# The last four experts of a mixture-of-experts layer, with expert 31's gate and up moved to the front

## The reference, cut to what matters

```python
for e in range(N_EXPERTS):
    hid = jax.nn.silu(t @ w_gate[e]) * (t @ w_up[e])
    out = out + combine[:, e:e + 1] * (hid @ w_down[e]).astype(f32)
```

## Time and profile before

| | |
|---|---|
| median of 3 runs | 1825.13 us (1824.73 to 1826.35) |
| the profiled execution | 1825.3 us, its span 1823.3 us |
| TensorE busy | 1663.8 us (91% of the span) |
| VectorE, ScalarE busy | 1034.6 and 387.7 us |
| mean granted clock of TensorE | 0.973 |
| the experts, in the 40 slices of the page | from slice 30 on the transfers run at 420 to 434 GB/s nearly throughout |

### The profile page before, as it was taken

One profiled execution on the slowest core, in us unless ns is written; L12 is line 12 of the kernel. 1 busy time (PEld: TensorE's weight loads), 2 busy tenths in 40 slices (PEclk: granted clock), 3 DMA queues, 4 the chain that ended last, 5 costly groups with the idle time before them and its releaser, 6 DMA issues.

```text
span 1823.3 us, 34390 instructions
## 1 busy us (share of the span) xinstructions
PE 1663.8 (91%) x14856; PEld 1334.9 (73%) x14856; DVE 1034.6 (57%) x2175; ACT 387.7 (21%) x993; POOL 0.2 (0%) x4
## 2 busy tenths in 40 slices
PE   7999999999999999999999999999998766566766
PEld 4555686888888886776899998778787555445554
DVE  1399979888867427787699884556433211111112
ACT  0254414211220104222322212203502100000001
POOL 0000000000000000000000000000000000000000
PEclk9999999999999999999999999999999978888899
DMA  9423334223240313744434443332398999999997
GB/s 383 180 82 115 110 135 162 105 112 129 104 150 24 127 47 137 268 164 162 174 139 180 185 168 139 139 122 104 137 421 320 431 434 426 432 431 431 431 426 298
DMA packets 30421, 395.00 MB, mean 217 GB/s; under 512 B 3296, under 2 KB 6624, under 8 KB 14432
## 3 DMA queue, kind: packets, MB, share of 16 engines
q1 hardware_dynamic: 30304, 393.31, 53.4%
HBM read 392.25 MB, written 1.05 MB: 216 GB/s over the span
## 4 chain that ended last, share of the span: by engine, by line
PE 82%; DMA 14%; DVE 3%; issue 1%; ACT 0%; SPq 0%; DVEq 0%
PE bank L2161 14%; PE bank L1871 13%; DMA arena<-w_moe 12%; PE bank L731 12%; PE bank L1599 7%; PE bank L4115 5%; PE bank L2438 3%; PE bank L2484 3%; PE bank L1029 2%; PE bank L4126 2%; PE bank L3869 2%; PE bank L2434 2%; PE bank L1334 1%; PE bank L785 1%; DMA ring<-w_moe 1%; PE bank L3091 1%
## 5 line engine op out<-in xcount | busy, mean ns | idle before, releaser
L1871 PE MATMUL bank<-arena,ring 128*128 128x256 f32 (+1 forms) x940 | 167.4, 336 | 0.0
L1871 PEld LDWEIGHTS bank<-arena,ring 128*128 128x128 f32 x940 | 148.0, 191 | 14.5 <-issue 0.4
L4115 PE MATMUL bank<-arena 128*32 128x128 f32 x1992 | 80.2, 332 | 76.9 <-DMA arena<-w_moe 73.4
L4281 DVE TENSOR_TENSOR arena<-arena,bank 128x128 f32<-128x128 f32 x32 | 9.2, 287 | 235.3 <-PE bank L4115 235.1
L4115 PEld LDWEIGHTS bank<-arena 128*32 128x32 f32 x1992 | 71.2, 137 | 84.3 <-DMA arena<-w_moe 77.5
L2161 PE MATMUL bank<-arena 128*128 128x256 f32 x504 | 115.7, 379 | 0.0
L731 PE MATMUL bank<-layer_input,ring 128*128 128x256 f32 x496 | 111.5, 381 | 0.0
L2161 PEld LDWEIGHTS bank<-arena 128*128 128x128 f32 x504 | 95.7, 190 | 13.2 <-DVE arena L2302 0.2
L731 PEld LDWEIGHTS bank<-layer_input,ring 128*128 128x128 f32 x496 | 92.8, 190 | 15.0 <-issue 2.8
L4115 PE MATMUL bank<-ring,arena 128*32 128x128 f32 x1920 | 64.8, 299 | 27.9 <-DMA ring<-w_moe 26.7
L4115 PEld LDWEIGHTS bank<-ring,arena 128*32 128x32 f32 x1920 | 59.2, 121 | 34.1 <-DMA ring<-w_moe 28.1
(11 more groups left out here) (572 smaller groups left out, 3162.1 us busy)
## 6 DMA issues: line engine op xcount, KB each, us to landing
arena<-w_moe SPq DMA_DIRECT2D x11, 6144.0 KB, 20.0
ring<-w_moe SPq DMA_DIRECT2D x11, 6144.0 KB, 20.4
ring<-w_ffn_in SPq DMA_DIRECT2D x13, 2048.0 KB, 7.6
ring<-w_moe SPq DMA_DIRECT2D x12, 2048.0 KB, 16.4
ring<-w_ffn_in SPq DMA_DIRECT2D x7, 3072.0 KB, 10.3
ring<-w_proj SPq DMA_DIRECT2D x7, 3072.0 KB, 9.8
arena<-w_moe SPq DMA_DIRECT2D x10, 2048.0 KB, 14.8
ring<-w_ffn_out SPq DMA_DIRECT2D x6, 2816.0 KB, 9.6
```

The source lines that it names most:

```text
L1871: last = eng.matmul(out, w[:, k * P:(k + 1) * P], x[:, k, :], start=(start and k == 0), stop=(stop and k == half - 1), skip_group_check=True)
L4115: ins = eng.matmul(bank[x][group[q], 0:P], xe[:, k, SLOTS * e:SLOTS * e + SLOTS], weight(e, first, last, (x * KT + k) * FE + q * P, P), st ...
```

## The change

In the last quad TensorE now begins with expert 31's gate and up, before the scatter of the quad before it; the turned hidden rows of expert 31 go to a place of their own (`last_hidt`, in `self.A`) and wait there for the down at the end. The scatter at expert 30 stands ahead of its gate. VectorE's and ScalarE's programs for the last quad are written out in the same order. The rest of expert 31's up is loaded ahead of the loop, to a sixth place (`up2`, in `self.A`). Its down goes to the place that held expert 2's down: three quarters in one transfer, the last quarter in 16 transfers of 8 partitions each. Eight fills are put ahead of the down of 29 and of 30, behind the wait for the copied rows and ahead of the wait for the weights; two fills ahead of each lone scatter. In the first attention the fills at the last pair go from 8 to 14.

```diff
-        sp.wait_ge(parts_used[1], LAST - 1)
-        self.load_part(sp, LAST, 0, 1, HELD_UP)
-        sp.wait_ge(parts_used[2], LAST - 1)
         self.load_last_down(sp)
...
+        self.load_held(sp, "up2", UPS // 2 + HELD_UP, UPS)
         with sp.Fori(0, (PARTS_AGAIN - WHOLE_FROM) // 2) as it:
...
-                sp.wait_ge(used, x - 1)
+                sp.wait_ge(used, x - 1 + (x == LAST - 1 and part < 2))
                 self.load_part(sp, x, (x - RESIDENT - 1) % 2, part)
...
+        place, split = self.kept_weights()["down"], (FET - 1) * D
+        sp.dma_start(place[:, 0:split], self.W["moe"][LAST][:, UPS:UPS + split]).then_inc(self.sem("first_in"), 16)
+        for r in range(0, P, 8):
+            sp.dma_start(place[r:r + 8, split:], self.W["moe"][LAST][r:r + 8, UPS + split:])\
+                .then_inc(self.sem("kept_in"), 16)
...
-                self.fill(pe, 8, b)
+                self.fill(pe, 14, b)
...
+            def last_quad(i):
+                x0, z = i * QUAD, QUAD - 1
+                project(0, z, last=True, copied=i * 2 + 1).then_inc(s["gate_done"], 1)
+                eng.wait_ge(self.sem("kept_in"), 9 * 16)
+                project(1, z, last=True).then_inc(s["up_done"], 1)
+                eng.wait_ge(s["y_dve"], x0 + 1)
+                eng.wait_ge(s["y_act"], x0 + 1)
+                for t in range(2):
+                    scatter(t)
+                eng.wait_ge(s["hid_ready"], x0 + 1)
+                eng.transpose(bank[3][:, 0:P], v["hid"], self.con("ident")).then_inc(s["hid_turned"], 1)
+                for e in range(z):
...
+                    if e == 2:
+                        eng.wait_ge(s["gwt_copied"], i * 2 + 2)
+                        eng.wait_ge(s["y_dve"], x0 + 3)
+                        eng.wait_ge(s["y_act"], x0 + 3)
+                        for t in range(2):
+                            scatter(t)
+                    eng.wait_ge(gate_in, arrived)
+                    project(0, e).then_inc(s["gate_done"], 1)
...
+                    eng.wait_ge(s["hidt_copied"], x0 + e + 2)
+                    eng.wait_ge(s["y_dve"], x0 + e + 1)
+                    eng.wait_ge(s["y_act"], x0 + e + 1)
+                    if e:
+                        self.fill(eng, 8, bank[0])
+                        eng.wait_ge(down_in, 64)
+                    down(e, False, True)
...
+                self.fill(eng, 2, bank[0])
+                eng.wait_ge(s["y_dve"], EXPERTS)
+                eng.wait_ge(s["y_act"], EXPERTS)
+                scatter_alone(2, 0)
+                eng.wait_ge(link, quads + 4)
+                scatter_alone(2, 1)
+                eng.wait_ge(self.sem("first_in"), 48)
+                down(z, False, True)
...
-            quad(quads - 1, last=True)
+            last_quad(quads - 1)
+            self.fill(eng, 2, bank[0])
             eng.wait_ge(s["y_dve"], EXPERTS + 1)
```

More of the change, by code:

```diff
@@ L4100, in weight @@
                 return self.kept_weight(at, n)
-            if last and e == QUAD - 1 and at < UPS // 2 + HELD_UP:
+            if last and e == QUAD - 1:
                 return self.held_weight(at, n)
@@ L4120, in down @@
         def down(e, first, last):
+            rows = last_hidt if last and e == QUAD - 1 else hidt
             for f in range(FET):
                 if last and e == QUAD - 1 and f == FET - 1:
-                    eng.wait_ge(self.sem("kept_in"), 9 * 16)
+                    eng.wait_ge(self.sem("kept_in"), (9 + P // 8) * 16)
                 for g in range(4):
-                    ins = eng.matmul(bank[2][group[g], 0:256], hidt[:, SLOTS * f:SLOTS * f + SLOTS],
+                    ins = eng.matmul(bank[2][group[g], 0:256], rows[:, SLOTS * f:SLOTS * f + SLOTS],
                                      weight(e, first, last, UPS + f * D + (g - e) % 4 * 256, 256), start=(f == 0),
@@ L4159, in moe, with quad @@
         if who == "pe":
-            def quad(i, first=False, second=False, last=False):
+            def quad(i, first=False, second=False):
                 x0 = i * QUAD
@@ L4223, in quad @@
                         eng.wait_ge(down_in, parts)
-                    down(e, first, last)
-                    if e == QUAD - 1 and not last:
+                    down(e, first, False)
+                    if e == QUAD - 1:
                         gather(i + 2)
@@ L4252, in moe, with silu, quad, last_quad @@
         if who == "act":
-            def quad(i, last=False):
+            def silu(n):
+                eng.wait_ge(s["gate_done"], n + 1)
+                eng.activation(v["sg"], bank[0][:, 0:P], ACT.Silu).then_inc(s["silu_done"], 1)
+            def quad(i):
                 for e in range(QUAD):
                     x = i * QUAD + e
-                    eng.wait_ge(s["gate_done"], x + 1)
                     if e:
                         eng.wait_ge(s["hid_ready"], x)
-                    eng.activation(v["sg"], bank[0][:, 0:P], ACT.Silu).then_inc(s["silu_done"], 1)
-                    if last and e == 2:
-                        eng.wait_ge(s["down_done"], x + 1)
+                    silu(x)
+                    copy_rows(x, e, eng.copy, (2, 3), "y_act")
+            def last_quad(i):
+                x0 = i * QUAD
+                silu(x0)
+                for e in range(QUAD - 1):
+                    eng.wait_ge(s["hid_ready"], x0 + e + 1)
+                    silu(x0 + e + 1)
+                    if e == 2:
+                        eng.wait_ge(s["down_done"], x0 + e + 1)
                         eng.copy(alone[e][64:128, :], bank[2][64:128, 0:256]).then_inc(s["y_act"], 1)
-                    elif not last or e < 2:
-                        copy_rows(x, e, eng.copy, (2, 3), "y_act")
+                    else:
+                        copy_rows(x0 + e, e, eng.copy, (2, 3), "y_act")
             eng.nop().then_inc(s["y_act"], 1)
@@ L4268, in moe @@
                 quad(i)
-            quad(quads - 1, True)
+            last_quad(quads - 1)
         if who == "dve":
@@ L4304, in quad @@
+            def quad(i):
+                weights(i)
+                one_hots(i + 1)
                 for e in range(QUAD):
                     x = i * QUAD + e
-                    hidden(x)
-                    if last and e == 2:
-                        eng.wait_ge(s["down_done"], x + 1)
-                        eng.tensor_copy(alone[e][0:64, :], bank[2][0:64, 0:256]).then_inc(s["y_dve"], 1)
-                    elif last and e == QUAD - 1:
-                        eng.wait_ge(s["down_done"], x + 1)
-                        eng.tensor_copy(alone[e], bank[2][:, 0:256]).then_inc(s["y_dve"], 1)
-                    else:
-                        copy_rows(x, e, eng.tensor_copy, (0, 1), "y_dve")
@@ L4315, in quad, with last_quad @@
-                    if e == QUAD - 1 and not last:
-                        copy_xe(i + 2, (0, 1))
-                    if last and e == 0:
+                    hidden(x, hidt)
+                    copy_rows(x, e, eng.tensor_copy, (0, 1), "y_dve")
+                    if e == QUAD - 1:
+                        copy_xe(i + 2, (0, 1))
+                    if e < 2:
+                        turned_weights(i, e)
+            def last_quad(i):
+                x0 = i * QUAD
+                weights(i)
+                hidden(x0, last_hidt)
+                eng.tensor_tensor(gains.rearrange("p (k c) -> p k c", k=KT),
+                                  self.con("ident").unsqueeze(1).to_broadcast([P, KT, P]),
+                                  self.vec("final_norm").unsqueeze(2).to_broadcast([P, KT, P]), ALU.mult)\
+                    .then_inc(self.sem("y_used"), 1)
+                for h in range(2):
+                    eng.wait_ge(self.sem("y_ready"), self.GAINS_SPREAD + h)
+                    eng.tensor_copy(final_gain[:, 512 * h:512 * h + 512], bank[3][:, :])\
+                        .then_inc(self.sem("y_used"), 1)
+                for e in range(QUAD - 1):
+                    hidden(x0 + e + 1, hidt)
+                    if e < 2:
+                        copy_rows(x0 + e, e, eng.tensor_copy, (0, 1), "y_dve")
+                    if e == 0:
```

115 lines of the change are left out of this document (52 added, 63 removed).

## The result

The changed kernel takes 1828.86 us, the median of 11 runs (1826.78 to 1831.18); the kernel before, run beside it on the same chip, takes 1824.73 (11 runs). The ratio is 1.0027, with a 95% interval of 1.0018 to 1.0036: 3.3 to 6.6 us slower. The interval lies clear of 1, so the change made the kernel slower; the median lies above the 0.2% that the prediction drew as its line, while the lower end of the interval, 0.18%, lies just under it. The profiled execution took 1828.63 us, of which 1826.9 are span.

A forecast was written before the change was run, and what follows sets the result against it. The weight stream was taken to bound the loop, and TensorE's work and waits for its own results the last quad. 0.6 - 0.3 + 3.6 = +3.9 us gave 1829.2 profiled, median 1829.0; range 1826.3 to 1831.5.

The forecast's parts named there:

- Fills in the last waits: Ahead of the downs of 29 and 30: two groups of eight fills, both paid in full, 2 x 1.78 = +3.6 us.
- Rival 1: Last quad: part of the fills is covered, one 1.78 disappears, +2.1 us, 1827.2; chance 0.18.
- The new order: Last quad, expert 31's gate and up at the front: waits gained and lost add up to -0.3 us.
- the 0.44 of issue: Expert 29's up: the idle time put down to issue, 0.44 us, assumed to be met again.
- The stream: Loop: 256 KB moved ahead of it make experts 7 to 30 land later, last quad begins 0.60 later, +0.6 us.
- The short fills: Two fills ahead of each lone scatter, 0.45 us, fit into the 0.55 wait for the copy: 0 (to +0.3).
- the attention's fills: First attention, 8 to 14: six more fills, 1.34 us, lie in a 1.79 us wait for VectorE: 0 (to +1.3).
- The small transfers: Last quarter of expert 31's down in 16 transfers: lands at about 1810, before TensorE asks at 1815; no cost.
- rival 3: End of last quad: small transfers land late, at 1827.9, the down ends 16.1 us later, 1841; chance 0.08.
- Rival 2: Waits for down weights: the stream bounds the end, fills cost nothing, -0.8 to -2.0 us, some 1823.7; chance 0.06.

The follow-up runs named there:

- e1: The changed kernel without the last quad's fills (8, 8, 2 and 2): 1825.95 us, ratio 1.0004 to the kernel before.
- e2: The kernel before, its order kept, with eight fills ahead of the down of 29 and of 30: 1827.19 us, ratio 1.0012 to the kernel before.
- e4: The changed kernel with the fills at the first attention's last pair back at 8: 1829.43 us, ratio 1.0030 to the kernel before.
- e5: The changed kernel with one more transfer of 2 MB ahead of the loop: 1834.85 us, ratio 1.0054 to the kernel before.
- e3: The changed kernel with the last quarter of expert 31's down in one transfer: 1829.75 us, ratio 1.0032 to the kernel before.
- e6: e1 with the scatter at expert 30 behind its gate: 1825.85 us, ratio 1.0006 to the kernel before.
- e7: e6 with the last quarter of expert 31's down in one transfer: 1823.84 us, ratio 1.0001 to the kernel before.
- e9: e8 with the last quarter of the down in 16 small transfers again: 1825.84 us, ratio 1.0004 to the kernel before.
- e8: e7 with the gains' two spreads at the front and the scatter behind expert 30's up: 1824.40 us, ratio 0.9999 to the kernel before.

## Why the prediction was right

1829.0 was forecast and 1828.86 measured, and the price stood where it was put: from the gather to the last down 3.6 - 0.3 = 3.3 us were forecast and 3.23 measured. That the medians agree to 0.14 us is luck. Runs of one kernel differ by 4 us, the kernel before came out at 1824.73 and not at the 1825.13 that the forecast starts from, and terms that were off stand against each other: the fills 0.4 dearer, the new order 0.4 cheaper, and the 0.6 of the stream not to be told from the noise at the end. Point by point:

- *Fills in the last waits, +3.6.* Right in place and sign, a little small: 1.99 + 1.98 = 3.97. A group holds the engine for 16 passes of 0.124 on average; the 1.78 was 2.05 less one of the 275 ns that a pass lasts from start to end, but the passes overlap, so only about 0.06 of the last one is hidden. e1 took the cost away and e2 showed when it is not there. Rival 1 (part covered) falls, as both groups were paid in full, with no wait for weights behind either.
- *The new order, -0.3.* It counted the 0.44 of issue as met again, and that is the term that was off: in the changed kernel the gap is gone, and expert 29 takes 4.25 us from its gate to its turn where it took 4.83 (1784.58 to 1789.41 before, 1788.36 to 1792.61 after). Without the gap the same sum gives -0.3 - 0.44 = -0.74, and -0.74 is what the trace shows. The other parts are as laid out: no wait for 30's gate, 1.10 at the scatter, 1.19 behind up 30, 0.58 ahead of the lone scatter. In these profiles the gap goes with eight fills in the attention and not with the order (e4); why was not tested.
- *The stream, +0.6.* Of the right size near its start, but not to be seen where I had said it would be. Expert 27 started 0.48 earlier, not 0.6 later. From the end of the first gather to expert 7 it is 1466.51 - 1388.79 = 77.72, against 1467.70 - 1390.67 = 77.03 before: +0.69. The other profiles agree: 77.0 us in both of the old order, 77.2 to 78.0 in the nine of the new order without e5. What hid it ahead of that is the first gather, which lay 0.25 earlier and took 3.81 instead of 5.44 us; it took 5.44 in five of the twelve profiles and 3.81 in seven. Behind expert 7 it cannot be followed: from the end of the first gather to the last it is 376.53 us before, but 378.71 in e2, whose program is the same up to there, and 377.9 to 378.6 in those nine. The sum took the one execution of before as fixed. That bytes ahead of the loop are paid at all rests on e5.
- *The short fills, 0, and the attention's fills, 0.* Both right where they stand: they replace a wait for VectorE that is as long as they are or longer (0.58 and 1.79). That the attention's fills may also have taken the gap of issue out of expert 29 was in nobody's sum.
- *The small transfers, 0.* Right for this kernel, because the fills push the last down behind them; rival 3, at 1827.9, was far off. The Trainium skill's rule on the page "DMA: Bandwidth & Descriptors", section "Why a DMA increments its semaphore by 16 and not by 1", put the last landing near 1811, and it came at 1811.09; that agreement is luck. With one transfer the landing comes 40.87 us after the gather (e3), which is 1807.9 on this clock, and the small ones are 44.0 - 40.9 = 3.2 us later, where half the engines on 512 KB would explain 1.2 by that rule, an estimate; the rest is open. The trace does agree with the rule's steps: each of these transfers brought 8 of its 16 steps of the semaphore as it landed, and the others as it was issued. The same page of the Trainium skill, section "Rules for kernel authors", calls transfers under 64 KB mostly overhead and has them joined. The trace agrees: e6 and e7 are 1.44 us apart. But the 2 us each that the prediction set beside it, which the page fits on transfers issued by GpSimd, did not add up here: sixteen took 5.75 us of SyncE to issue and were all in 1811.09 - 1788.74 = 22 us after the first issue, with the megabytes queued ahead of them.
- *Rival 2 (the stream becomes the bound)* did not come true in the changed kernel, since the fills pushed TensorE behind the weights. Where the fills were gone, it did: in e1, e6 and e9 the end hung on the last landing, and in e8 expert 30's up stood 1.29 us before its weights.

The failures are among the expectations. In e8 I had counted the covered chains as gained without asking which landing would be late next; and e1, e3 and e7 had the landing of the last quarter wrong, in one transfer 1 to 2 us too late (e3), and so the difference between the two ways as 1 to 1.3 us (e7).

## What to carry to other kernels

A fill that stands behind the last wait ahead of a matmul is paid in full, as both groups were here, however idle the engine looks in the chart; it is free only as far as another wait follows it. Read which wait ends last before and behind the place, and work out what landing comes due next before counting a covered wait as won: in this quad, without the fills, TensorE and the stream lie within 2 us of each other. Where what comes ahead of a stage moves by 2 us from one execution to the next, compare the stage from its own first instruction.

## What the runs showed of the hardware that was not expected

- Sixteen transfers of 8 partitions and 32 KB, behind a full queue, landed 3.2 us later than the same 512 KB in one transfer of 128 partitions (44.0 against 40.9 us after the gather; 44.1 against 40.7 in e6 and e7).
- The same 32 matmuls of the first gather took 5.44 us in some executions and 3.81 in others. The granted clock was 1.00 in the 85 us ahead of it in both, with TensorE busy for 83.5 and 83.3 of them; in the slow ones it fell during the gather, as the stretch around it shows, before and then after:

```profile
1385.00:1391.00 6.00, 5.77 (x48) 5.68 (x52) 2.40 (x14) 1.79 (x4) 0.00 (x0) 0.72 0.43 151
```

```profile
1385.00:1391.00 6.00, 6.00 (x118) 5.81 (x122) 3.83 (x22) 2.04 (x5) 0.00 (x0) 1.00 0.45 145
```

- In the loop the granted clock was 0.88 before and 0.81 after (1600 to 1700 us), and the rounds were as long (29.07 and 29.08 us between two starts that wait for weights, 1613.94 to 1643.01 in the trace of before and 1613.44 to 1642.52 in that of after): where the stream was the bound, the clock cost nothing.
- Idle time put down to issue stood at the same instructions in two executions of one program, and at others in a program with twelve passes fewer ahead of it: behind pass 88 of expert 29 in the kernel before and e2, behind pass 87 in e4, nowhere in expert 29 in the two profiles of the changed kernel.
